# The sync engine waits for the scatters itself; GpSimd and ScalarE take parts of the closing sums

## The reference

```python
w = jnp.take_along_axis(s, eidx, axis=-1)              # 8 experts per token
w = w / jnp.sum(w, axis=-1, keepdims=True) * ROUTED_SCALE
...
y = jnp.einsum('nef,efd->nd', hid, lp['w_down'])       # weighted sum of the 8 experts' results
sh = (jax.nn.silu(x @ lp['w_sh_gate']) * (x @ lp['w_sh_up'])) @ lp['w_sh_down']
...
h = h + g2 * y                                         # second residual, y with the shared part
y = xf * lax.rsqrt(jnp.mean(xf * xf, axis=-1, keepdims=True) + EPS) * g   # final norm
```

## Time and profile before

| | us |
|---|---|
| three runs | 1094.63, 1096.72, 1097.2 |
| the profiled execution | 1096.59 |
| its span, from the first to the last instruction | 1094.8 |
| PE busy | 1043.3 (95%) |
| DVE busy | 533.0 (49%) |
| ACT busy | 357.3 (33%) |
| POOL busy | 157.0 (14%) |

### The profile page before, as it was taken

How to read it: one execution, slowest core, us unless ns; L and a number is a source line. 1 busy time by engine, 2 the same in 40 slices (tenths; PEclk the granted TensorE clock), 3 DMA queues, 4 the chain that set the end, 5 groups by cost and what they waited for, 6 DMA issues and landing times.

```text
span 1094.8 us, 15005 instructions
## 1 busy us (share of the span) xinstructions
PE 1043.3 (95%) x4876; PEld 699.7 (64%) x4876; DVE 533.0 (49%) x1118; ACT 357.3 (33%) x481; POOL 157.0 (14%) x136
## 2 busy tenths in 40 slices
PE   4999999999899999999989999999999999999975
PEld 2599988789788897874645455555555555454532
DVE  1523544445798956945634334433344334333357
ACT  3334444327444445501423222223223222222201
POOL 0020321000000000000010323322322213221000
PEclk9999999999999999999999999999999999999998
DMA  9999775447544323740297999999999999999592
GB/s 387 413 265 395 103 98 92 156 154 258 206 173 154 151 82 98 250 151 1 97 372 272 379 407 397 421 408 396 418 419 424 401 406 421 417 410 411 224 411 104
DMA packets 54912, 306.61 MB, mean 280 GB/s; under 512 B 12550, under 2 KB 16902, under 8 KB 35920
## 3 DMA queue, kind: packets, MB, share of 16 engines
q1 hardware_dynamic: 35280, 270.63, 61.3%
q0 software_dynamic: 12256, 26.80, 10.5%
q10 hardware_dynamic: 7328, 8.55, 2.3%
HBM read 285.31 MB, written 36.85 MB: 294 GB/s over the span
## 4 chain that ended last, share of the span: by engine, by line
PE 58%; DMA 2%; DVE 2%; ACT 1%; issue 1%; DVEq 0%; SPq 0%
PE PS L2056 16%; PE PS L2058 8%; PE PS L2081 4%; PE PS L1945 4%; PE PS L2042 3%; PE PS L1693 3%; PE PS L2071 2%; DMA bigA<-in_w_down 2%; PE PS L2073 2%; PE PS L2072 2%; PE PS L2013 2%; PE PS L2130 1%; PE PS L1935 1%; PE PS L1933 1%; PE PS L1934 1%; PE PS L2097 1%
## 5 line engine op out<-in xcount | busy, mean ns | idle before, releaser
L1093 POOL DMA_INDIRECT y_parts<-bigB,IDX x38 | 73.9, 1944 | 327.2 <-DVE bigB L1630 318.1
L2056 PE MATMUL PS<-bigB 128*128 128x512 f32 x224 | 101.7, 597 | 0.0
L1747 PE MATMUL PS<-bigB_r 128*128 128x384 f32 x288 | 98.5, 342 | 1.3 <-ACT bigB L779 1.3
L1749 PE MATMUL PS<-bigB_r,bigA_r 128*128 128x384 f32 x288 | 96.5, 335 | 0.0
L1748 PE MATMUL PS<-nT_r,bigB_r 128*128 128x384 f32 x288 | 96.3, 334 | 0.0
L1630 DVE TENSOR_SCALAR bigB<-PS,bigD 128x1024 f32<-128x1024 f32 x40 | 51.3, 1283 | 90.2 <-PE PS L2073 55.5
L2058 PE MATMUL PS<-bigA,bigB 128*64 128x512 f32 x208 | 94.8, 598 | 0.5 <-issue 0.5
L2059 PE MATMUL PS<-bigB 128*64 128x512 f32 x208 | 94.8, 598 | 0.0
L2056 PE MATMUL PS<-bigA,bigB 128*128 128x512 f32 x208 | 94.6, 598 | 0.0
L1238 DVE TENSOR_TENSOR bigA_r<-bigA,bigB_r 128x2048 fp32r<-128x2048 f32 x18 | 41.3, 2293 | 97.6 <-ACT bigB_r L805 97.6
L1596 DVE TENSOR_TENSOR bigB<-bigB,PS 128x256 f32<-128x256 f32 x40 | 16.9, 421 | 138.1 <-ACT bigB L989 138.0
(11 more groups left out here) (370 smaller groups left out, 2117.9 us busy)
## 6 DMA issues: line engine op xcount, KB each, us to landing
bigB<-in_w_gu SPq DMA_DIRECT2D x27, 2048.0 KB, 17.6
bigA<-in_w_gu SPq DMA_DIRECT2D x26, 2048.0 KB, 15.1
bigA<-in_w_in SPq DMA_DIRECT2D x17, 2048.0 KB, 10.0
bigB<-in_w_down SPq DMA_DIRECT2D x27, 1024.0 KB, 17.9
bigA<-in_w_down SPq DMA_DIRECT2D x26, 1024.0 KB, 18.0
bigA<-in_w_ada SPq DMA_DIRECT2D x8, 2048.0 KB, 9.0
y_parts<-bigB SPq DMA_DIRECT2D x6, 2048.0 KB, 30.1
bigB<-in_w_ada SPq DMA_DIRECT2D x3, 2048.0 KB, 20.2
```

Of the source, the lines that this page charges most:

```text
L1093: pool.indirect_dma_start(y_parts, bass.IndirectOffsetOnAxis(ap=IDX[:, p, 1:2], axis=0), YS[:, p % 2, :], None, bounds_check=T * TOPK - 1, ...
L1747: mm(out, wh, nh, start=(k == 0), stop=False)
L1749: last = mm(out, wl, nh, start=False, stop=(k == KD - 1))
L2056: last = mm(PS[:, 2 + b, :], XT[:, b, k, :], GU_W[s][:, :, k, :], start=first, stop=stop)
```

## The change

It has four parts.

1. SP waits for the scatters itself. The constants get two more columns beside that of the unit numbers, with the value that each of the two scatter semaphores reaches in the end. DVE multiplies three columns where it multiplied one, PE turns two more of them into rows in the stage "row", and DVE copies the two largest values to ROW after it has raised `row_done`, and raises it again. SP reads both values into registers behind the first six weight transfers, and at the end waits for `scat[0]` and `scat[1]` to reach them. POOL no longer waits and `added` is gone.
2. POOL adds the two rows of chunks 3, 7, 10 and 11 in place, each as soon as its chunk has been loaded, and DVE adds the sum in one operation.
3. PE no longer adds chunk 9; DVE does, as the first chunk of tile 2.
4. The last product of tile 0 leaves DVE: ACT multiplies by the factor and POOL by FG. SP waits for POOL there.

```diff
     put(K_COL, np.stack([r, unit] + [SCAT0 + 16 * (np.maximum(unit - 1 - b, 0) // 2) for b in range(2)], 1))
...
             units = unit_count(sp)
+            sp.wait_ge(row_done, 2)
+            landed = [sp.value_load(ROW[0:1, RTAB + 1 + b:RTAB + 2 + b], ...) for b in range(2)]
...
-            sp.wait_ge(added, 2)
+            for b in range(2):
+                sp.wait_ge(scat[b], landed[b])
...
             for m in range(NT):
-                sp.wait_ge(fin_done, m + 1)
+                if m == 0:
+                    sp.wait_ge(ho_root, NT + 1)
+                else:
+                    sp.wait_ge(fin_done, m)
...
+                if m == 0:
+                    act.wait_ge(ho_ms, NT + 1)
+                    nc.scalar.activation(YN[:, 0, :], XH[:, 0, :], ACT.Identity, scale=small[:, 12:13]).then_inc(ho_taken, 1)
...
-                with pool.Else():
-                    pool.wait_ge(scat[p % 2], pas * (16 * BODY // 2) + (scat0 + 16 * (p // 2)))
-                    pool.sem_inc(added, 1)
...
+            for i in (3, 7, 10, 11):
+                pool.wait_ge(y_back[i], 32 if i < EARLY else 16)
+                nc.gpsimd.tensor_tensor(YG[i][:, 0, :], YG[i][:, 0, :], YG[i][:, 1, :], ALU.add).then_inc(pair_sum, 1)
+            pool.wait_ge(fin_loaded, 64)
+            pool.wait_ge(ho_taken, NT + 1)
+            nc.gpsimd.tensor_tensor(YN[:, 0, :], YN[:, 0, :], FG, ALU.mult).then_inc(ho_root, 1)
...
                     nc.vector.tensor_copy(ROW[0:1, 0:RTAB], PS[0:1, 1, 0:RTAB]).then_inc(row_done, 1)
+                    link(nc.vector.tensor_reduce(RC[0:1, 9:11], PS[0:1, 1, 2 * RTAB:4 * RTAB]..., AX.X, ALU.max))
+                    nc.vector.tensor_copy(ROW[0:1, RTAB + 1:RTAB + 3], RC[0:1, 9:11]).then_inc(row_done, 1)
...
+                    if i in (3, 7, 10, 11):
+                        dve.wait_ge(pair_sum, (3, 7, 10, 11).index(i) + 1)
+                        link(nc.vector.tensor_tensor(ACC, ACC, YG[i][:, 0, :], ALU.add))
+                        continue
...
+                if m == 0:
+                    dve.sem_inc(ho_ms, 1)
+                    return
                 nc.vector.scalar_tensor_tensor(YN[:, m, :], XH[:, m, :], col(12), FG, ALU.mult, ALU.mult).then_inc(fin_done, 1)
...
-            rows_of(2, (2, 3))
+            rows_of(2, (1, 2, 3))
...
                     mm(PS[0:1, 1, 0:RTAB], NCNT, ident, start=True, stop=True)
+                    for i in range(2):
+                        mm(PS[0:1, 1, (2 + i) * RTAB:(3 + i) * RTAB], RC[:, 1 + i:2 + i], ident, start=True, stop=True)
                     mm(PS[0:1, 1, RTAB:2 * RTAB], RC[:, 0:1], ident, start=True, stop=True).then_inc(pr_ready, 1)
...
-            loaded_rows(2, 0, False, False)
-            loaded_rows(2, 1, False, True).then_inc(part_ready, 1)
+            loaded_rows(2, 0, False, True).then_inc(part_ready, 1)
```

More of the change, by code:

```diff
@@ L55 @@
 NOWHERE = 4096
+SCAT0 = 64 * (NH // 2)
 TAIL_BANK = (0, 2, 6)
@@ L60 @@
 K_ID, K_SEL, K_MASK, K_LEV, K_SCAN, K_TRI, K_ONE, K_R128, K_TOK, K_COL, K_T8, K_END, K_SUB = range(13)
-K_W = [P, 2 * P, GRID_W, 7 * P, T, P, P, P, NT * 4, 2, NG * NG, 0, RTAB]
+K_W = [P, 2 * P, GRID_W, 7 * P, T, P, P, P, NT * 4, 4, NG * NG, 0, RTAB]
 K_AT = [sum(K_W[:i]) for i in range(14)]
@@ L89, in shape_constants @@
     r = np.arange(RTAB)
-    put(K_COL, np.stack([r, np.where(r < BIG0, r // 2 * 3 + 3, (r - BIG0) // 2 * 3 + r % 2 + 1)], 1))
+    unit = np.where(r < BIG0, r // 2 * 3 + 3, (r - BIG0) // 2 * 3 + r % 2 + 1)
+    put(K_COL, np.stack([r, unit] + [SCAT0 + 16 * (np.maximum(unit - 1 - b, 0) // 2) for b in range(2)], 1))
     put(K_SUB, np.tile(np.where(r < BIG0, r % 2 * HALF - 1, -1 - P * (r - BIG0))[None].astype(np.float32), (P, 1)))
@@ L453, in trunk @@
         ho_ready = sem("hgrn_out_ready")
-        ho_taken = sem("hgrn_out_copied")
-        ho_ms = sem("hgrn_mean_square")
-        ho_root = sem("hgrn_root")
+        ho_taken = sem("hgrn_out_copied_then_final_scaled")
+        ho_ms = sem("hgrn_mean_square_then_final_scale")
+        ho_root = sem("hgrn_root_then_final_product")
         ho_norm = sem("hgrn_normed")
@@ L472, in trunk @@
         rows_go = sem("row_transfer_may_start")
-        added = sem("all_results_written")
+        pair_sum = sem("row_pairs_summed_then_final_products")
         sh_loaded = sem("shared_weights_loaded")
@@ L523, in trunk @@
         ys_done = sem("results_weighted")
-        scat, scat0 = in_bias, 64 * (NH // 2)
+        scat, scat0 = in_bias, SCAT0
         y_back = [sem(f"early_ada_then_parts_loaded_{m}") for m in range(4 * NT)]
@@ L667, in _ @@
             units = unit_count(sp)
+            sp.wait_ge(row_done, 2)
+            landed = [sp.value_load(ROW[0:1, RTAB + 1 + b:RTAB + 2 + b], min_val=SCAT0, max_val=SCAT0 + 16 * UNITS_MAX) for b in range(2)]
             sp.wait_ge(shd_ready, NT)
@@ L1557, in _ @@
                     nc.vector.tensor_tensor(SE, SE, TMP.unsqueeze(1).broadcast_to([P, NT, NE]), ALU.add)
-                    link(nc.vector.tensor_reduce(RC[:, 0:1], EON, AX.X, ALU.add))
-                    nc.vector.tensor_tensor(RC[:, 0:1], RC[:, 0:1], kc(K_COL)[:, 1:2], ALU.mult)
+                    link(nc.vector.tensor_reduce(RC[:, 4:5], EON, AX.X, ALU.add))
+                    nc.vector.tensor_scalar(RC[:, 0:3], kc(K_COL)[:, 1:4], RC[:, 4:5], None, ALU.mult)
                     link(nc.vector.tensor_tensor(TMP, EON, kc(K_R128)[:, 0:NE], ALU.mult))
@@ L1564, in _ @@
                     dve.wait_ge(pr_ready, 1)
-                    link(nc.vector.tensor_reduce(RC[0:1, 1:2], PS[0:1, 1, RTAB:2 * RTAB], AX.X, ALU.max))
-                    link(nc.vector.tensor_copy(ROW[0:1, RTAB:RTAB + 1], RC[0:1, 1:2]))
+                    link(nc.vector.tensor_reduce(RC[0:1, 8:9], PS[0:1, 1, RTAB:2 * RTAB], AX.X, ALU.max))
+                    link(nc.vector.tensor_copy(ROW[0:1, RTAB:RTAB + 1], RC[0:1, 8:9]))
                     nc.vector.tensor_copy(ROW[0:1, 0:RTAB], PS[0:1, 1, 0:RTAB]).then_inc(row_done, 1)
+                    link(nc.vector.tensor_reduce(RC[0:1, 9:11], PS[0:1, 1, 2 * RTAB:4 * RTAB].rearrange("p (a r) -> p a r", a=2), AX.X, ALU.max))
+                    nc.vector.tensor_copy(ROW[0:1, RTAB + 1:RTAB + 3], RC[0:1, 9:11]).then_inc(row_done, 1)
                 elif st == "table":
```

## The result

The kernel after takes 1099.61 us in the median of seven runs (1098.59 to 1104.55), beside 1095.71 for the kernel before in seven runs beside it (1094.63 to 1097.2). The ratio is 1.0038, with a 95% interval of 1.0022 to 1.0055: slower by 2.4 to 6.0 us. The forecast was 1100.7, within 1093.8 to 1102.6. The profiled execution took 1099.63, its span 1097.8 where that of before was 1094.8.

A forecast was written before the change was run, and what follows sets the result against it. The prediction took the later of two closing chains, PE's and DVE's, half a microsecond apart, as the bound. With DVE shut out, +3.65 + 0.4 = +4.1 us on 1096.59 gave 1100.7, range 1093.8 to 1102.6.

The forecast's parts named there:

- The sync engine's wait: SP's wait before the first chunk: removing the detour over POOL gives 0; two more matmuls in stage "row" cost +0.4 us.
- The mechanism: Closing sums: DVE's second SBUF input and POOL's reads go one at a time, so DVE waits a whole POOL addition.
- The branch without hold-up: Closing sums if POOL doesn't disturb DVE: residual 2 starts at 1079.8 in place of 1082.55, -2.8 us.
- P: Length of one POOL pair addition of 1024 columns: taken as 2.5 us, bounds 0.735 and 2.94.
- Pair 7: POOL's addition of chunk 7: gets in at 1063.0, holds residual 0's second operation to 1065.5; residual 0 ends 1068.0, not 1066.8.
- Pairs 10 and 11: POOL's additions of chunks 10 and 11: run to 1073.05 and 1075.7, holding final 0's small operations until 1076.25.
- The product: POOL's product with FG, 1077.4 to 1079.9: holds the second operation of residual 1 from 1077.5 to 1079.9.
- some 6.4 us: Closing sums: the prediction's figure for how long DVE's chain is shut out.
- Rival 1: Closing sums: DVE isn't held up, -2.8 + 0.4 = -2.4 us, 1094.2; chance 0.27.
- Rival 2: Closing sums: the engines share in part, half the loss, +0.5 + 0.4 us, 1097.5, no change; chance 0.11.
- 3: Whole kernel faster by more than the bound: no hold-up, "row" matmuls covered by slack, -3.4 us at most, 1093.2; chance 0.05.
- Rival 4: End of the kernel: the direct wait brings the loads forward, worth under 0.1 us; no chance given.

The follow-up runs named there:

- part 1 alone: Kernel before with only the sync engine's wait changed (SP waits for the scatters itself, with its columns, matmuls and register loads): median 1096.67 us, ratio 0.9990.
- The kernel with one pair: Kernel after, but POOL adds only chunk 3's pair and keeps tile 0's product; DVE adds chunks 7, 10 and 11: median 1098.14 us, ratio 1.0003.
- the early pairs: Kernel before, with POOL adding the pairs of chunks 1 to 4 before DVE's additions and chunk 4 moved from PE to DVE: median 1094.80 us, ratio 0.9960.
- the write-only kernel: Kernel after, with POOL's four pair additions replaced by memsets of 2048 columns: median 1095.58 us, ratio 0.9996.
- The one-input kernel: Kernel after, with POOL's four pair additions replaced by multiplications of one row by 2.0: median 1096.72 us, ratio 0.9993.
- tile 0's product on DVE: Kernel after, with the last product of tile 0 back on DVE as one operation and the four pairs kept on POOL: median 1100.26 us, ratio 1.0015.

## Why the prediction was right

**The sync engine's wait.** Costed at 0 at the end and 0.4 us in the stage "row". Measured: PE still last at the end, and +0.49 (+0.50 with part 1 alone). The two matmuls are 0.44 as worked out; the rest stands in the row in front of them (0.37 in place of 0.31), which the prediction left out. That the 0.5 us reaches the end is not shown.

**The mechanism.** The prediction inferred from one side (POOL's scatters wait for DVE) that DVE would wait for POOL in the same way. The trace of after shows it four times. The kernel with one pair and the early pairs show that it goes away where the two don't meet, and the write-only kernel that it takes POOL's reading. The one-input kernel sets a limit to it: there the hold-up ends long before POOL's row does. What the prediction inferred for additions is therefore shown for additions and products of two inputs, and a hold-up for the whole length isn't true of every POOL operation that reads. The branch without hold-up was right too, as the write-only kernel shows: the arithmetic on the earlier trace rows held to 0.1 us, and only the choice between the branches was a matter of judgment.

**P.** I took 2.5 us, from 256 columns scaled up with DVE's fixed part. It is 2.34. The estimate of 2.35 that the prediction has from the Trainium skill's "GPSIMD Engine Reference" was the better figure; a straight line between the page's 4497 ns for 2048 columns and this case's 735 ns for 256 gives it.

**Where the pairs fall.** The stretch came out at 28.02 where the steps gave 28.2, but by errors that cancel. Pair 7 was to get in at the seam in front of the PSUM operation of residual 0 and cost 1.2 us. It came at 1060.99, one operation earlier, and cost 2.03. DVE's first addition begins 19.01 us behind the first chunk's fetch in both traces, but pair 7 began 22.45 us behind it, where I had 23.1. Pairs 10 and 11 were to cost 4.25 together and cost 2.03 + 1.34 = 3.37, since pair 10 came in under an addition of tile 1. The product was put at 2.4 and cost 2.18. Together the steps held 7.85 us of hold-up, and 7.58 were measured. The prediction calls it "some 6.4 us"; that is the difference to the branch without hold-up, in which DVE waits 1.4 us for PE. As the sum of what DVE is held for, the figure is wrong by these 1.4.

**The sum.** +3.65 + 0.4 against +3.47 + 0.49: 4.1 predicted, 3.96 read from the traces, 3.90 between the medians. The base was the profiled execution of before with 1096.59; the seven runs beside the kernel after have a median of 1095.71, and that 0.9 is most of why 1100.7 was a little high. The interval of the time, 2.4 to 6.0 us slower, excludes rivals 1 and 2 (-2.4 and +0.9), but it also holds the +5.9 of P = 2.94; it is the rows that tell the terms.

**The rivals.** Rival 1 (DVE not held) and 3 fall with the four long rows. Rival 2 (shared in part) falls for additions, where DVE is shut out until 0.14 us before POOL's end; for a one-input operation something like it is true. Rival 4 falls with SP's wait for PE.

## What to carry to other kernels

Before work goes from DVE to POOL, look at what DVE runs at that moment: beside two-input additions in SBUF a pair on POOL took 2.03 us from DVE to save it 1.25, while a version with as many pairs, all done before DVE's additions began, shortened the stretch by 2.8 us. Where two chains end within half a microsecond of each other, ask of each edit which of them it lengthens; part 3 here put an addition on the chain that became the bound. An engine that is shut out shows as busy, so compare each row's length with the same operation elsewhere, and a small operation in the way of a long one is held just as long.

## What the runs showed of the hardware

- A DVE operation with two SBUF inputs waits for a POOL addition or product of two SBUF inputs that takes 2.34 us: 1.22 became 3.25 and 3.40, 0.16 became 1.50 and 2.35. Operations with one input beside the same POOL rows kept their time: TENSOR_SCALAR 0.15 at 1072.93 and RECIPROCAL 0.16 at 1073.42 in the kernel after, and so did those that read PSUM (1.23 at 1062.54 with tile 0's product on DVE).
- A POOL multiplication with one input took 2.77 us and held DVE for only 0.71 to 0.79. The Trainium skill ("SBUF — State Buffer", section "Who interferes with whom") calls the shared pair an exclusive lock, held for the whole instruction; it says the latter of DVE's two-port modes, and the prediction took it for every contention. For this operation the measurement says otherwise, and the measurement decides. Why the length differs was not tried.
- A POOL memset of 2048 columns took 1.80 us and held nobody: two-input DVE operations that began beside it took 0.16 and 1.23.
- POOL waits too. In the kernel before, 19 of the 38 scatters took 2.87 to 2.90 us, and each of them began beside a DVE operation of 2.28 or 2.29 us with two SBUF inputs; the other 19 took 0.98 to 1.02.
- PE's granted clock fell (0.57 and 0.61 in the 4 us that followed) behind an idle time of 2.52 us in two kernels (16 matmuls in 8.83 and 8.69 us), and not behind 1.20 to 1.63 in the other seven (7.13 us). That is worth 1.7 us in the closing sums, and it came where the last unit's products had taken 5.49 us and not 4.21 to 4.61. How much of the spread between executions comes from it stays open, since only the profiled one of each kernel has a trace.
